# Column sums of squares in a decoder block: f32 matmuls with ones replaced by a bf16 high part and a bf16 low part

## The reference

```python
def rms_norm(x, g):
    y = x * lax.rsqrt(jnp.mean(x * x, axis=-1, keepdims=True) + EPS)
    return y * g

u = rms_norm(h, g_attn);  z = u @ w_in
ya = swa_sink_attention(...)     # 16 heads, window 128, sinks, QK-norm
yd = diff_attention(...)         # 8 differential heads, dense causal, QK-norm, sub-norm
h = h + concat([ya, yd]) @ w_out
u2 = rms_norm(h, g_ffn)
h = h + (silu(u2 @ w_gate) * (u2 @ w_up)) @ w_down         # d_ff = 5632
gate = sigmoid(rms_norm(h, g_ple) @ w_ple_gate)
h = h + gate * rms_norm(p @ w_ple_proj, g_ple_out)
```

## Time and profile before

| | us |
|---|---|
| median of 3 runs | 3387.06 (3377.00 to 3532.3) |
| the profiled execution | 3378.32 |
| its span on the slowest core (core 6) | 3376.8 |
| spans of the 8 cores | 3356.6 to 3376.8 |
| PE busy | 3185.9 (94%) |
| DVE / ACT / POOL busy | 1212.9 / 918.4 / 528.4 |
| f32 matmul records with ones | 40, 24.1 us busy |

### The profile page before, as it was taken

One profiled execution on the slowest core, in us unless ns is written; L12 is line 12 of the kernel. 1 busy time (PEld: TensorE's weight loads), 2 busy tenths in 40 slices (PEclk: granted clock), 3 DMA queues, 4 the chain that ended last, 5 costly groups with the idle time before them and its releaser, 6 DMA issues.

```text
span 3376.8 us, 47907 instructions; the slowest of 8 cores (3356.6 to 3376.8 us)
## 1 busy us (share of the span) xinstructions
PE 3185.9 (94%) x17170; PEld 1575.7 (47%) x17500; DVE 1212.9 (36%) x2255; ACT 918.4 (27%) x1630; POOL 528.4 (16%) x508
## 2 busy tenths in 40 slices
PE   5887989999889999999999999999999999999998
PEld 2443655555444444444444444444444444444444
DVE  6775655555553112222222100022222221000555
ACT  4475456666665221000000010110000000011111
POOL 4523111111101330000000011100000000111333
PEclk8999999999999999999999999999999999999999
DMA  8221211110333774444444666454444436555863
GB/s 216 78 48 27 47 31 23 22 32 8 75 119 83 214 212 91 75 75 76 78 79 85 145 159 154 115 99 80 79 76 76 75 67 123 139 129 126 230 175 109
DMA packets 80550, 333.59 MB, mean 99 GB/s; under 512 B 8288, under 2 KB 16736, under 8 KB 60480
## 3 DMA queue, kind: packets, MB, share of 16 engines
q0 software_dynamic: 24160, 177.68, 30.2%
q1 hardware_dynamic: 56160, 152.83, 13.6%
HBM read 441.04 MB, written 66.58 MB: 150 GB/s over the span
## 4 chain that ended last, share of the span: by engine, by line
PE 82%; DVE 7%; issue 4%; DMA 4%; ACT 2%; POOL 1%; DVEq 0%; SPq 0%; ACTq 0%; POOLq 0%
PE psall L203 82%; DVE arena L229 3%; DVE arena L226 2%; ACT arena L223 2%; DMA arena<-w_down 2%; DMA arena<-xT 1%; DMA arena<-vbuf 1%; PE psall L207 0%; DVE sm L233 0%; POOL arena L676 0%; DVEq L102 0%; DVE sm L760 0%; SPq L237 0%; DVE arena L466 0%; POOL arena L226 0%
## 5 line engine op out<-in xcount | busy, mean ns | idle before, releaser
L203 PE MATMUL psall<-arena 128*128 128x512 bf16 (+3 forms) x16680 | 3119.9, 345 | 111.9 <-DVE arena L226 37.0
L203 PEld LDWEIGHTS psall<-arena 128*128 128x128 bf16 x17004 | 1535.8, 98 | 1681.5 <-issue 177.2
L226 DVE TENSOR_TENSOR arena<-psall,arena 128x512 f32<-128x512 f32 x677 | 450.8, 687 | 1707.9 <-PE psall L203 1610.5
L223 ACT ACTIVATE arena<-arena 128x512 f32<-128x512 f32 (+2 forms) x608 | 401.3, 671 | 1407.9 <-DVE arena L226 1352.6
L223 ACT ACTIVATE arena<-psall 128x512 bf16<-128x512 f32 (+5 forms) x888 | 451.3, 549 | 316.2 <-PE psall L203 280.2
L226 POOL TENSOR_TENSOR arena<-arena 128x512 f32<-128x512 f32 (+2 forms) x252 | 381.3, 1514 | 932.9 <-ACT arena L223 324.0
L223 ACT ACTIVATE arena<-arena,cstt 128x1024 bf16<-128x1024 f32 x64 | 73.5, 1148 | 704.6 <-DVE arena L226 704.6
L226 DVE TENSOR_TENSOR arena<-arena 128x512 bf16<-128x512 f32 (+2 forms) x304 | 230.0, 757 | 73.8 <-ACT arena L223 56.2
L237 POOL DMA_DIRECT2D arena<-w_gate x44 | 23.4, 531 | 817.4 <-PE psall L203 796.6
L229 DVE SCALAR_TENSOR_TENSOR arena<-psall,cstt,arena 64x512 bf16<-64x512 f32 (+1 forms) x136 | 101.6, 747 | 24.2 <-ACT arena L223 19.6
L226 DVE TENSOR_TENSOR arena<-arena,cb 128x128 bf16<-128x128 bf16 x256 | 54.9, 228 | 123.5 <-ACT arena L223 115.0
(11 more groups left out here) (46 smaller groups left out, 285.2 us busy)
## 6 DMA issues: line engine op xcount, KB each, us to landing
arena<-w_gate POOLq DMA_DIRECT2D x44, 1024.0 KB, 9.7
arena<-w_up POOLq DMA_DIRECT2D x44, 1024.0 KB, 9.2
arena<-w_down POOLq DMA_DIRECT2D x32, 1408.0 KB, 12.1
hbuf<-arena SPq DMA_DIRECT2D x64, 512.0 KB, 10.7
arena<-hbuf SPq DMA_DIRECT2D x64, 512.0 KB, 11.4
arena<-w_in POOLq DMA_DIRECT2D x17, 1024.0 KB, 8.7
arena<-xT SPq DMA_DIRECT2D x16, 1024.0 KB, 9.7
arena<-xT SPq DMA_DIRECT2D x32, 512.0 KB, 6.4
```

The lines of the kernel that those rows point to most:

```text
L203: p.op('pe', lambda e: e.matmul(out, lhsT=lhsT, rhs=rhs, start=start, stop=stop, skip_group_check=skip), reads, writes)
L223: p.op('act', lambda e: e.activation(out=out, in_=in_, func=func, **kw), reads, writes)
L226: p.op(eng, lambda e: e.tensor_tensor(out=out, in0=in0, in1=in1, op=op), reads, writes)
```

## The change

The stationary tile of ones becomes bf16 (`ones_b`). What is summed is split on DVE into a high part, the value cast to bf16, and a low part, the difference to it, also in bf16; two bf16 matmuls into one PSUM bank add both. In `stats_fin`, DVE first adds `accP` to `accD`, then casts and subtracts. In the three groups the splits (`split2`, two DVE operations each, four of them) are put earlier in the text than the matmuls: in group A between the forced `run_dfr(True)` and the last k-steps of n = 0, in groups B and C ahead of the 32 matmuls that precede the group.

```diff
-        ones_f = T("ones_f", [128, 128], F32)
+        ones_b = T("ones_b", [128, 128], BF16)
@@
-        p.op('dve', lambda e: e.memset(ones_f[:], 1.0), [], ['ones_f'])
+        p.op('dve', lambda e: e.memset(ones_b[:], 1.0), [], ['ones_b'])
@@ def stats_fin(tc):
             s_ = sbank()
-            MM(ps[s_], ones_f[:], accD.ap, True, False, ['ones_f'] + accD.all(), [PSR[s_]])
-            MM(ps[s_], ones_f[:], accP.ap, False, True, ['ones_f'] + accP.all(), [PSR[s_]])
+            hi, lo = Buf(118, [128, 512], BF16), Buf(119, [128, 512], BF16)
+            TT(accD.ap, accD.ap, accP.ap, ALU.add, accD.all() + accP.all(), accD.all())
+            p.op('dve', lambda e: e.tensor_copy(out=hi.ap, in_=accD.ap), accD.all(), hi.all())
+            TT(lo.ap, accD.ap, hi.ap, ALU.subtract, accD.all() + hi.all(), lo.all())
+            MM(ps[s_], ones_b[:], hi.ap, True, False, ['ones_b'] + hi.all(), [PSR[s_]])
+            MM(ps[s_], ones_b[:], lo.ap, False, True, ['ones_b'] + lo.all(), [PSR[s_]])
             ACT(rtx.ap, ps[s_], AF.Ln, [PSR[s_]], rtx.all(), scale=1.0 / D, bias=EPS)
             ACT(rtx.ap, rtx.ap, AF.Exp, rtx.all(), rtx.all(), scale=-0.5)
@@
-        def ones_rstd(acc_ap, acc_pg, bank, out_ap, out_pg):
-            MM(ps[bank][:], ones_f[:], acc_ap, True, True, ['ones_f'] + acc_pg, [PSR[bank]])
+        def split2(ap, pg, o1, o2):
+            hi, lo = Buf(o1, [128, 512], BF16), Buf(o2, [128, 512], BF16)
+            p.op('dve', lambda e: e.tensor_copy(out=hi.ap, in_=ap), pg, hi.all())
+            TT(lo.ap, ap, hi.ap, ALU.subtract, pg + hi.all(), lo.all())
+            return hi, lo
+
+        def ones_rstd(hl_, bank, out_ap, out_pg):
+            hi, lo = hl_
+            MM(ps[bank][:], ones_b[:], hi.ap, True, False, ['ones_b'] + hi.all(), [PSR[bank]])
+            MM(ps[bank][:], ones_b[:], lo.ap, False, True, ['ones_b'] + lo.all(), [PSR[bank]])
@@ group A, output projection, n == 0, pr == 0
                         run_dfr(True)
+                        sp2 = [split2(pss[i].ap, pss[i].all(), 152 + 2 * i, 153 + 2 * i) for i in range(4)]
                     oproj(15, pr, bb)
                     if pr == 1:
                         for i in range(4):
                             sl = rstd3.cols(i * 512, i * 512 + 512)
-                            ones_rstd(pss[i].ap, pss[i].all(), (4, 5, 6, 7)[i], sl[0], sl[1])
+                            ones_rstd(sp2[i], (4, 5, 6, 7)[i], sl[0], sl[1])
@@ group B, ahead of the gate matmuls of f = 0
+                    if hf == 0 and f == 0:
+                        sp2 = [split2(rA(i * 512, i * 512 + 512), rAp(i * 512, i * 512 + 512), 152 + 2 * i, 153 + 2 * i)
+                              for i in range(4)]
@@
-                                ones_rstd(sl[0], sl[1], 4 + i, sl[0], sl[1])
+                                ones_rstd(sp2[i], 4 + i, sl[0], sl[1])
@@ group C, ahead of the matmuls of step 0
+            if i == 0:
+                sp2 = []
+                for j in range(4):
+                    ra, rp = rstd2.cols(j * 512, j * 512 + 512)
+                    sp2.append(split2(ra, rp, (148, 150, 168, 170)[j], (149, 151, 169, 171)[j]))
@@
-                    ones_rstd(ra, rp, 4 + j, ra, rp)
+                    ones_rstd(sp2[j], 4 + j, ra, rp)
```

## The result

The changed kernel takes 3396.86 us (median of 22 executions) against 3387.29 for the kernel before (22 executions). The ratio is 1.0047, with a 95% interval of 1.0034 to 1.0060: slower by 0.0047 x 3387 = 16 us, where 6.6 were forecast (the two medians, which are over all executions, differ by 9.6). The ratios here leave out executions in which a whole die ran at a lower clock than the other. In the profiled execution the slowest core is core 4 with 3392.9 us.

The account below looks back on a forecast made before the run. PE was taken to bound the kernel, with 82% of the chain, except where it waits. Terms +3.8 (stats_fin), +1.4 and +1.7 (group A), -0.3 (B) and 0 (C) gave +6.6 on 3378.3: 3385 us, range 3370 to 3398.

Parts of the forecast that it names:

- the sum's own high end of +12: Whole kernel: the high bounds of all terms together, 6 + 1.9 + 1.7 + 2.0 + 0.5 us.
- The term for the latency in `stats_fin`: Four input-norm sums: added DVE work delays ACT by 0.3, 1.7, 0.9 and 0.9 us; +3.8, bounds +1.5 to +6.
- Stream prices: PE's stream: an f32 matmul takes 0.86 us, two bf16 ones 0.43, bf16 starts being 0.22 apart.
- The serial part in stats_fin: stats_fin: DVE add, cast, subtraction and last matmul stand serially before ACT, taking 2.65 to 2.9 us.
- Group A: Sums near 1060 us: splits delay DVE adds by 1.5 us, PE resumes +1.4 later, clock fall costs 1.7 more.
- Group B: Sums near 1279 us: PE gains only 0.3 us instead of 1.7, because the splits come too slowly.
- Group C: Sums ahead of step 2, near 3140 us: effect 0, since PE waits for `vbuf` anyway; bound +0.5.
- The stream gain (1): Rival, all sums: splits hidden, PE's stream counts; at most -10.3 us, or -7.8 with waits kept (3370.5); chance 0.17.
- Absorption (2): Rival, first 150 us and attention: later waits absorb everything; 3378, between -1 and +2 us; chance 0.20.

Follow-up runs that it names:

- e1: The change in stats_fin alone, groups A, B and C as in the kernel before; +8.0 / +7.9 us (slower / faster core) against before, ratio 1.0019.
- e2: The change in groups A, B and C alone, stats_fin with f32 matmuls as before; +0.6 / +1.6 us against the kernel before, ratio 1.0003.
- e7: Kernel before with stats_fin alone as single bf16 matmuls, last adds writing bf16, no split or low part; -1.8 / -1.5 us against before, ratio 0.9988.
- e11: The changed kernel without the low part in stats_fin (add, cast, one bf16 matmul); +4.8 / +5.0 us against the kernel before, ratio 1.0027.
- e3: The changed kernel measured again, no edit, on another chip; +8.4 / +10.0 us against the kernel before, too few executions for a ratio.
- e10: The changed kernel measured once more, no edit, for spread and slow-clock cores; +8.6 / +7.6 us against the kernel before, ratio 1.0045.
- e5: Kernel before with all sums as single bf16 matmuls, last adds writing bf16, no split or low part; -3.7 / -4.1 us against before, ratio 0.9981.
- e9: Direct bf16 sums everywhere, no splits, input norm's last two tiles swapped between GpSimd and VectorE; -3.5 / -3.8 us against the kernel before, ratio 0.9988.

## Why the prediction was wrong

It forecast +6.6 us, with 3385 in a range of 3370 to 3398. The direction was right, and so was the place of the largest term, `stats_fin`; the effect measured is +16 us (11.5 to 20), beyond the sum's own high end of +12. That 3396.9 lies in the range is no merit of the sum: the range had been made wider for the spread between executions. Two steps failed. The term for the latency in `stats_fin`, +3.8, was too small: alone it measured +8. And the sum had no term for a granted clock of 0.81, which adds 11 to 12 us to the cores that get it and is about the other half of the 16. Point by point:

- **Stream prices: right.** 32 matmuls with `ones_b`; the five in a row of group B (below) take 1.24 us, that is (1.24 - 0.38) / 4 = 0.22 apart.
- **The serial part in stats_fin: right in length, wrong in price.** Chunk 2 took 2.87 us as said. In chunk 1 the new add met POOL and took 1.63 us instead of 0.69, as its row of 1.33 had suggested; the Trainium skill (SBUF — State Buffer, Who interferes with whom) describes such exclusion, and this row agrees with it:
```profile
60.33 1.15 POOL L226 TENSOR_TENSOR arena<-arena 128x512 bf16<-128x512 f32 x1
60.39 1.63 DVE L226 TENSOR_TENSOR arena<-arena 128x512 f32<-128x512 f32 x1
```
  But "the latency is the cost" (+3.8) is the term that was too small: `stats_fin` alone measured +8 (e1). The prediction added 0.3, 1.7, 0.9 and 0.9 us for chunks 0 to 3; by e1 against e2 they are -0.6, 2.3, 2.5 and 1.6, which is 5.9 at the last sum. It weighed the new serial part only from the end of the two STT to ACT and took the time from one sum to the next partial sums as unchanged. In chunk 2 the first is right. POOL's adds (before, core 6; changed kernel, core 4):
```profile
85.39 8.10 POOL L226 TENSOR_TENSOR arena<-arena 128x512 bf16<-128x512 f32 x5
88.32 7.40 POOL L226 TENSOR_TENSOR arena<-arena 128x512 bf16<-128x512 f32 x5
```
  ACT starts 3.4 us behind their end (95.72 to 99.08) instead of 2.3 (93.49 to 95.78), +1.1. The rest is made in front of it: from chunk 1's ACT start (64.18, before 63.40) to the end of POOL's adds it is 31.5 us and was 30.1. And nothing was said of the attention stage, where e1 loses 3.6 us more.
  A reason that fits is the clock. TensorE's waits at the sums of chunks 1 to 3 are 6.8, 5.5 and 5.5 us in e1 (means of eight cores) and 2.3, 3.0 and 2.2 in e2, and the mean granted clock from 50 to 160 us is 0.90 and 0.93. I charged the clock in group A, from a row of chunk 2, and did not charge it in the chunks themselves, where that row stood. That the added latency is handed on from chunk to chunk is measured (e7, e11, e1); that the clock is the reason for what goes beyond the serial part is argued from the rows, since no run changes the clock alone.
- **The clock level of 0.81: not seen at all.** No stretch of the trace before has it. It is about half of the measured 16 us: undisturbed pairs with the change are 8 to 10 us above before (e3, e10), and pairs with this level are 11.5 us longer still in the first measurement, 12 in e10. The slowest core sets the time, so that one such pair is enough.
- **Group A: right.** The adds start 4.87 us behind the copy instead of 3.67, PE resumes 1.2 us later (1.4 said), and the clock falls (0.90 in 17 us, e2: 1.7 us, as said). The stretch around it is 2.6 us longer in e2 and 3.2 in e10, where 1.4 + 1.7 = 3.1 were forecast. In the time at the end it can't be told from the spread.
- **Group B: right.** The last two low parts wait for DVE L226, 1.1 us apart (changed kernel, core 4):
```profile
1303.98 1.24 PE L203 MATMUL psall<-arena,ones_b 128*128 128x512 bf16 x5
1305.55 0.71 PE L203 MATMUL psall<-arena,ones_b 128*128 128x512 bf16 x2 [0.33 <-DVE arena L226]
1306.69 0.38 PE L203 MATMUL psall<-arena,ones_b 128*128 128x512 bf16 x1 [0.42 <-DVE arena L226]
```
  From ACT 1280 to ACT 1350 every core of the kernel before takes 333.3 us, every core with the splits 332.8 (-0.5, where -0.3 was forecast) and every core of e5, without them, 330.7.
- **Group C: right.** PE still waits for `vbuf` (changed kernel, core 4):
```profile
3148.08 5.00 PE L203 MATMUL psall<-arena 128*128 128x512 bf16 x16 [2.72 <-DVE arena L226]
3153.24 1.89 PE L203 MATMUL psall<-arena 128*128 128x512 bf16 x8 [0.17 <-DMA arena<-vbuf]
3156.20 9.01 PE L203 MATMUL psall<-arena 128*128 128x512 bf16 x41 [1.08 <-DMA arena<-vbuf]
```
- **Rivals.** The stream gain (1) is what e5 gets, where the splits are gone: -4, not -7.8. Absorption (2) does not happen in the chunks; a part of it does behind them (5.9 us at the last sum, 3.3 at ACT 200), and is lost again in the attention stage.

## What to carry to other kernels

A matmul made cheaper did not pay for work put between its last operand and itself: 1.3 us of TensorE saved in each sum were bought with 2.0 us of VectorE on the path. In this loop the added latency came back in full, chunk by chunk (8.3 us for 8.0), and the saved matmul time brought about 2 us in all. Where the precision allows it, let the producer write the narrow type instead of adding a cast. Where a wait of TensorE gets longer, ask at every such place what the granted clock behind it is, and what the delay does to the next round of the same loop.

## What was not expected of the hardware

With the change, single pairs of cores ran for 100 us and more in all at a granted clock of 0.81, between the two levels of 1.2 and 2.4 GHz, in executions whose other cores had 1.00 in the same stretch. The Trainium skill (TensorE: Matmul & The Clock Gate, Part 1: The HAM clock gate) tells of a limiter that takes a whole die to 13/16 of the clock, 0.8125, once three of its cores run dense matmuls. The level agrees with 0.81. The scope does not: in e10 cores 6 and 7 had it, and core 5 of the same die ran from 160 to 200 us at 1.00 (above). And the kernel before, with all eight cores busy, had mean clocks of 0.987 to 0.994. How often it came differed by chip: 37 of 70 pairs, none of 18, 5 of 20. What in the change brings it is open; e5, e7 and e9, without the added work, had it in none of their 100 pairs, and the kernel before had mean clocks as low in 2 of 230 pairs on the three later chips.
